# A hybrid diffusion layer on one core: TensorE's recurrence loop written out, and two small moves around it

## The reference, cut to what matters

```python
def wkv7_scan(r, w, k, v, a, b, s0, reverse):
    def step(S, inp):
        r_t, w_t, k_t, v_t, a_t, b_t = inp
        sa = jnp.einsum('bhvk,bhk->bhv', S, a_t)
        S = S * w_t[:, :, None, :] + sa[..., :, None] * b_t[..., None, :] + v_t[..., :, None] * k_t[..., None, :]
        return S, jnp.einsum('bhvk,bhk->bhv', S, r_t)
    ...
for d in range(2):
    ...
    kd = kh * (1.0 + (a - 1.0) * k_a)
    y, s_fin = wkv7_scan(rh, decay, kd, vh, -kk, kk * a, s0[d], reverse=(d == 1))
```

## Time and profile before

| | |
|---|---|
| time, median of three runs | 2733.13 us |
| the profiled execution's own time | 2725.9 us |
| its span (first to last instruction) | 2724.2 us |
| TensorE busy | 2289.1 us (84%), 26342 matmuls |
| VectorE busy | 1612.5 us (59%) |
| ScalarE busy | 1036.5 us (38%) |
| GpSimd busy | 233.0 us (9%) |
| mean granted TensorE clock | 0.931 |

### The profile page before, as it was taken

The page is one execution under the profiler, slowest core; times in us unless marked ns, Lnnn a source line. Parts: engine busy times, 40 slices in busy tenths (PEclk is TensorE's granted clock), DMA queues, the critical chain, the costliest instruction groups (busy, mean ns, idle before and its releaser), DMA issues. The chain is left out here.

```text
span 2724.2 us, 65696 instructions
## 1 busy us (share of the span) xinstructions
PE 2289.1 (84%) x26342; PEld 1857.7 (68%) x26342; DVE 1612.5 (59%) x2511; ACT 1036.5 (38%) x1760; POOL 233.0 (9%) x192
## 2 busy tenths in 40 slices
PE   5999999998999999996777777774553796798898
PEld 3788788886888888884666666663342574687687
DVE  6665665668654566664665666654675575677233
ACT  5443244444321244443444454442322664200222
POOL 0000000000000000003110001000000640200421
PEclk7999999999999999997899999997776898899899
DMA  6344333332333333332011111104335304676543
GB/s 217 115 134 121 93 116 118 102 119 96 111 100 98 97 116 102 114 107 79 28 44 37 37 37 37 48 23 133 125 119 162 118 3 129 235 265 236 177 139 123
DMA packets 263884, 300.23 MB, mean 110 GB/s; under 512 B 33274, under 2 KB 203386, under 8 KB 255482
## 3 DMA queue, kind: packets, MB, share of 16 engines
q1 hardware_dynamic: 261370, 288.65, 32.9%
q10 hardware_dynamic: 2304, 8.39, 0.8%
HBM read 194.62 MB, written 102.36 MB: 109 GB/s over the span
## 5 line engine op out<-in xcount | busy, mean ns | idle before, releaser
L715 PE MATMUL proj_ps<-h_hi,w_hi 128*128 128x512 f32 x1656 | 650.0, 393 | 28.2 <-DVE h_lo L465 20.3
L716 PE MATMUL proj_ps<-h_lo,w_hi 128*128 128x512 f32 x1656 | 647.3, 391 | 0.0
L717 PE MATMUL proj_ps<-h_hi,w_lo 128*128 128x512 f32 x1656 | 647.2, 391 | 0.0
L318 ACT CAST w_hi<-w_raw 128x512 fp32r<-128x512 f32 x420 | 255.1, 621 | 695.7 <-PE proj_ps L717 353.2
L715 PEld LDWEIGHTS proj_ps<-h_hi,w_hi 128*128 128x128 f32 x1656 | 312.6, 189 | 98.7 <-issue 27.2
L717 PEld LDWEIGHTS proj_ps<-h_hi,w_lo 128*128 128x128 f32 x1656 | 312.4, 189 | 65.9
L716 PEld LDWEIGHTS proj_ps<-h_lo,w_hi 128*128 128x128 f32 x1656 | 312.7, 189 | 63.4
L482 DVE TENSOR_TENSOR w_lo<-w_raw,w_hi 128x512 fp32r<-128x512 f32 x420 | 283.2, 689 | 44.0 <-ACT w_hi L318 43.7
L498 DVE TENSOR_TENSOR z_slots<-proj_ps,x_rows 128x512 f32<-128x512 f32 x174 | 120.3, 691 | 171.0 <-PE proj_ps L717 169.0
L498 DVE TENSOR_TENSOR x_rows<-proj_ps,x_rows 128x512 f32<-128x512 f32 x116 | 80.2, 691 | 109.7 <-PE proj_ps L717 103.8
L967 POOL TENSOR_TENSOR neighbours<-z_halo 128x1792 f32<-128x1792 f32 x9 | 28.8, 3200 | 1268.7 <-DMA z_halo<-scratch_zT 1268.7
(11 more groups left out here) (333 smaller groups left out, 3992.9 us busy)
## 6 DMA issues: line engine op xcount, KB each, us to landing
w_raw<-in_w_in SPq DMA_DIRECT2D x240, 256.0 KB, 3.0
scratch_gatesT<-z_slots SPq DMA_DIRECT2D x128, 256.0 KB, 2.7
m_gate<-scratch_gatesT SPq DMA_DIRECT2D x32, 1024.0 KB, 5.7
scratch_zT<-z_slots SPq DMA_DIRECT2D x108, 256.0 KB, 2.5
ada<-in_ada_w SPq DMA_DIRECT2D x4, 2048.0 KB, 15.4
mb_raw<-scratch_branchT SPq DMA_DIRECT2D x16, 512.0 KB, 5.6
scratch_mergedT<-m_y SPq DMA_DIRECT2D x8, 1024.0 KB, 5.7
y_raw<-scratch_mergedT SPq DMA_DIRECT2D x16, 512.0 KB, 4.9
```

The source lines that it names most:

```text
L318: A.copy(wh[:, i, :, :], raw[:, q, :, :]).then_inc(w_hi, 1)
L715: T.matmul(out, wh[:, i, k, :], hi[:, o, k, :], start=(first and k == 0), stop=False, skip_group_check=not first)
L716: T.matmul(out, wh[:, i, k, :], lo[:, o, k, :], start=False, stop=False, skip_group_check=not first)
L717: last = T.matmul(out, wl[:, i, k, :], hi[:, o, k, :], start=False, stop=(k == 3), skip_group_check=not first)
```

## The change

Four edits. TensorE no longer uses `units`: its program is 18 units in a row. VectorE's two halves of the states are split: the first half (P0, Q0) stays at the end of the unit, the second half (P1, Q1) comes behind the level-one mask of the next unit. TensorE's wait for Q1 moves accordingly, from ahead of X to between X and Z of level one. The turned rows of K in direction one move from level 3 to behind level 5, into PSUM bank 6, and ScalarE's copy of them moves behind the last Z. The names of the results are split to match (`tail_v`).

```diff
+            def states(n, d, c):
+                main_p.after(dve, n, f"PQ.{d}")
+                prep_a.after(dve, n, f"tot{d}")
...
+                done(V.tensor_tensor(to(Pst), pq[:, :, 0, :, :], eye, ALU.add), "P")
+                done(V.tensor_tensor(to(Qst), pq[:, :, 1, :, :], tt.to_broadcast([P, 2, 2, CH]), ALU.mult), "Q")
...
                     if v == 1:
+                        if d:
+                            states(n, 0, 1)
+                        elif not first_block(n):
+                            states(n - 1, 1, 1)
...
                 if nxt:
                     first_inverse(*nxt)
-                for c in range(2):
...
+                states(n, d, 0)
+                if nxt is None:
+                    states(n, d, 1)
```

ScalarE:

```diff
-                rows(Kt if d else Vt, "Kt." if d else "V.", "K." if d else "V.")
+                if d == 0:
+                    rows(Vt, "V.", "V.", 7)
...
                 factor(Z[:], "Z5.", 0)
-                if d == 0:
-                    rows(Kt, "Kt.", "K.")
+                rows(Kt, "Kt.", "K.", 6 if d else 7)
```

TensorE:

```diff
                         main_a.after(pe, n, f"Bt.{d}")
-                        if d:
-                            turned(lambda p: Kh[:, d, p, :], "K.")
-                        else:
+                        if d == 0:
                             turned(lambda p: zf[:, 4 + p, :], "V.")
...
-                        main_a.after(pe, n, f"Kt.{d}" if d else f"V.{d}")
+                        if d == 0:
+                            main_a.after(pe, n, "V.0")
...
                     if v == 1:
                         main_g.after(pe, n, f"Z.{d}")
                         before(main_a, "Y1.")
-                        before(main_v, "Q1.")
...
                         done(last, f"X{v}.")
+                    if v == 1:
+                        before(tail_v, "Q1.")
+                        go()
...
                 if d == 0:
                     prep_v.after(pe, n, "bt")
                     prep_p.done(mm(ps[:, 6, :], J[:], flat(kds[:])), "bonus")
+                else:
+                    turned(lambda p: Kh[:, d, p, :], "K.", 6)
                 main_a.after(pe, n, f"Z5.{d}")
...
                     if d == 0:
                         prep_v.after(pe, n, "bonus")
-                        main_a.after(pe, n, "Kt.0")
+                    main_a.after(pe, n, f"Kt.{d}")
                     first_inverse(*nxt)
...
-            units(pe, prologue, unit)
+            prologue()
+            for n in range(NBLK):
+                unit(n, 0, (n, 1))
+                unit(n, 1, (n + 1, 0) if n + 1 < NBLK else None)
```

More of the change, by code:

```diff
@@ L887, in recurrence_local_stage @@
         main_v = Results(ctx, nc, "main_vector", [f"{n}{d}" for d in range(2) for n in
-                         ["G1.", "MK.", "G2.", "G3.", "G4.", "G5.", "Gs0.", "Gs1.", "P0.", "Q0.", "P1.", "Q1."]])
+                         ["G1.", "MK.", "G2.", "G3.", "G4.", "G5."]])
+        tail_v = Results(ctx, nc, "tail_vector", [f"{n}{d}" for d in range(2) for n in ["Gs0.", "Gs1.", "P0.", "Q0.", "P1.", "Q1."]])
         head_v = Results(ctx, nc, "head_vector", ["MB.0", "X0.0", "MB.1", "X0.1"])
@@ L894, in recurrence_local_stage @@
         main_a = Results(ctx, nc, "main_scalar", [f"{n}{d}" for d in range(2) for n in
-                         ["X1.", "Z1.", "X2.", "Z2.", "Bt.", "X3.", "Z3.", "Kt." if d else "V.", "At.", "X4.", "Z4.", "MV.", "Z5."]
-                         + ["Kt."] * (1 - d) + ["W0.", "W1.", "Y0.", "Y1."]])
+                         ["X1.", "Z1.", "X2.", "Z2.", "Bt.", "X3.", "Z3."] + ["V."] * (1 - d)
+                         + ["At.", "X4.", "Z4.", "MV.", "Z5.", "Kt.", "W0.", "W1.", "Y0.", "Y1."]])
         prep_p = Results(ctx, nc, "prep_products", ["tw0", "ta0", "ks", "rnT", "tw1", "ta1", "bonus"])
         main_p = Results(ctx, nc, "main_products", [f"{n}{d}" for d in range(2) for n in
-                         ["G1.", "SK.", "X1.", "Z1.", "G2.", "B.", "X2.", "Z2.", "G3.", "K." if d else "V.", "X3.", "Z3.",
-                          "G4.", "A.", "X4.", "Z4.", "G5.", "MV."] + ["K."] * (1 - d) + ["Z5.", "W.", "GY.", "PQ."]])
+                         ["G1.", "SK.", "X1.", "Z1.", "G2.", "B.", "X2.", "Z2.", "G3."] + ["V."] * (1 - d) + ["X3.", "Z3.",
+                          "G4.", "A.", "X4.", "Z4.", "G5.", "MV."] + ["K.", "Z5."][::1 - 2 * d] + ["W.", "GY.", "PQ."]])
         head_p = Results(ctx, nc, "head_products", ["SB.0", "SM.0", "SB.1", "SM.1"])
@@ L943, in turn @@
                         load(n + 2)
-                    main_v.after(sp, n, f"Gs1.{d}")
+                    tail_v.after(sp, n, f"Gs1.{d}")
                     sp.dma_start(t["gT"][d, :, :, bass.ds(n * RB, RB)].rearrange("m p t -> p m t"), gst[:]).then_inc(g_stored, 16)
@@ L1121, in prologue @@
                     consts_set.step(dve, V.tensor_tensor(lev[:, d, 1:, :], lev[:, d, 1:, :], ident, ALU.add))
+            def states(n, d, c):
+                main_p.after(dve, n, f"PQ.{d}")
+                prep_a.after(dve, n, f"tot{d}")
+                done = lambda ins, name: tail_v.done(ins, f"{name}{c}.{d}")
+                pq = ps[:, c, :].rearrange("p (g q m j) -> p g q m j", g=2, q=2, m=2)
+                to = lambda st: st[:, d, bass.ds(n * 4, 4), :, :].rearrange("p (g c) m j -> p g c m j", c=2)[:, :, c, :, :]
+                tt = tot[:, d, bass.ds(n * 4, 4), :].rearrange("p (g c) (m o) -> p g c m o", c=2, o=1)[:, :, c, :, :]
+                eye = i64[:, :].rearrange("p (a b j) -> p a b j", a=1, b=1).to_broadcast([P, 2, 2, CH])
+                done(V.tensor_tensor(to(Pst), pq[:, :, 0, :, :], eye, ALU.add), "P")
+                done(V.tensor_tensor(to(Qst), pq[:, :, 1, :, :], tt.to_broadcast([P, 2, 2, CH]), ALU.mult), "Q")
             def unit(n, d, nxt):
@@ L1163, in unit @@
                     of_chunk = lambda a: a.rearrange("p m (g c t) -> p c g m t", g=2, c=2)[:, c]
-                    done(V.tensor_tensor(of_chunk(gst[:]), ps[:, 4 + c, 0:256].rearrange("p (g m t) -> p g m t", g=2, m=2),
-                                         of_chunk(AR[:, d, 1, :, :]), ALU.add), f"Gs{c}.")
+                    tail_v.done(V.tensor_tensor(of_chunk(gst[:]), ps[:, 4 + c, 0:256].rearrange("p (g m t) -> p g m t", g=2, m=2),
+                                         of_chunk(AR[:, d, 1, :, :]), ALU.add), f"Gs{c}.{d}")
                 if nxt:
                     first_inverse(*nxt)
-                main_p.after(dve, n, f"PQ.{d}")
-                prep_a.after(dve, n, f"tot{d}")
-                for c in range(2):
[L1171 to L1176, removed]
+                states(n, d, 0)
+                if nxt is None:
+                    states(n, d, 1)
             units(dve, prologue, unit)
@@ L1241, in factor, with rows @@
                     own(A.copy(to.rearrange("p q g m t -> p q (g m t)"), ps[:, bank:bank + 2, 0:256]), name)
-                def rows(to, name, sent):
+                def rows(to, name, sent, bank):
                     main_p.after(act, n, f"{sent}{d}")
-                    own(A.copy(flat(to[:]), ps[:, 7, :]), name)
+                    own(A.copy(flat(to[:]), ps[:, bank, :]), name)
                 if nxt and d:
@@ L1257, in unit @@
                 factor(Z[:], "Z2.", 0)
-                rows(Bt, "Bt.", "B.")
+                rows(Bt, "Bt.", "B.", 7)
                 if nxt and d:
@@ L1361, in before, with turned @@
                         results.earlier(pe, n, f"{name}1")
-                def turned(src, name):
+                def turned(src, name, bank=7):
                     for g in range(2):
@@ L1366, in turned @@
                             at = g * 256 + p * P
-                            last = T.transpose(ps[:, 7, at:at + P], src(p)[:, g * P:(g + 1) * P], s["ident"][:])
+                            last = T.transpose(ps[:, bank, at:at + P], src(p)[:, g * P:(g + 1) * P], s["ident"][:])
                     done(last, name)
```

## The result

The changed kernel took 2714.24 us (median of five, 2711.13 to 2717.56) beside 2733.13 us of the kernel before: ratio 0.9925, 95% interval 0.9907 to 0.9944, so 15 to 25 us, 20.5 by the ratio. Forecast: 2708, range 2688 to 2726. The profiled execution took 2714.24 us, that of before 2725.9: the two traces differ by 11.7 us only.

What follows compares the result with a forecast made beforehand. TensorE was taken as bound by its instruction supply, packets of some 256 about 3.3 to 4.3 us apart. Terms 16 + 5 + 3.5 = 24.5 us off the median 2733.1 gave 2708.6, forecast 2708, range 2688 to 2726.

Steps and rivals of the forecast that it cites:

- Part A: TensorE's loop written out, removing six back-edge jumps and no matmul: 16 us faster.
- Part B: States' second half moved behind the level-one mask, so TensorE waits less for VectorE's mask: 5 us faster.
- The clock's price: Granted clock falls behind each back-edge jump of TensorE's loop: 0.55 us per jump, 3.3 in all.
- a sign that I named: "Issue", TensorE's idle time waiting for nothing visible, 54.8 us in the loop's six pairs, lower by about 10 to 20.
- My upper bound: For Part A: all 20.3 us idle at the jumps goes, with the clock's price 23.6; 30 allowed.
- the lower bound: For Part B, TensorE's level-one mask waits: a gain of 0.
- Part C: Direction one's four K transposes leave level 3 for TensorE's idle time behind level 5: 3.5 us faster.
- R1: Written-out pairs idle like the first; packets swallow half the rest of Part B and Part C: 6 us, 2727; chance 0.16.
- R3: TensorE's stops vanish in written-out code: 67 us faster, 2666; chance 0.02.
- R4: Written-out packets come later from new addresses; at 0.9 us each the kernel is 24 us slower, 2757; chance 0.05.
- R5: Later stages' loops lie otherwise against packets' ends, possibly 3.4 us a turn; 8 us each way in the width.

Runs made afterwards that it cites:

- `micro`: Kernel before plus 2048 unread 64x64 products in TensorE's prologue, 1024 in a 16-turn loop, 1024 written out; profiled execution 2798.94 us.
- `a_only`: Kernel before with only TensorE's loop written out, VectorE and TensorE keeping their old order; 2713.49 us, ratio 0.992.
- the loop's experiment: Kernel before, loop kept, with only the states' second half moved behind level one's mask and TensorE's wait for Q1 with it; ratio 0.9994.
- `ac_out`: Changed kernel without the states' move: loop written out and K's rows moved; ratio 0.9902 against the kernel before.
- `ab_out`: Changed kernel with K's rows back at level 3: loop written out and states' move; ratio 0.9936 against the kernel before.

## Why the prediction was right or wrong

The direction, the range and the engine were right: 2714.24 in 2688 to 2726, 18.9 us by the medians where 24.5 were summed. The terms were less so: A was some 6 us too low and B at least 5 too high, and that these errors cancelled is luck.

- **What bounds the kernel.** Right, and measured alone by `micro`: instruction packets, one per 3.45 to 4.0 us where the code is dense, as the earlier trace rows had let me read (3.31 to 4.33), and 256 instructions to a packet, one weight load to a matmul (26342 of each on the page of before). Where TensorE waits for other engines, an end can pass without a stop: in the six pairs of `a_only` 10299 matmuls and 10293 weight loads are 80 packets, and it has 41 stops for "issue".
- **Part A, 16 us.** Too small: 22 (18 to 25) by the ratio. The term is the difference of two pairs in one trace, 62.0 and 59.35 us. Its written-out side was right: a pair of `a_only` takes 355.93 / 6 = 59.3 us, so between the two traces the stretch shrank by 16.1 us. What was mis-sized is the loop's side: it came from one execution, 7.2 us below the median of its five runs and 9 below that of the 29, and the sum carried this over as if it were a constant. In the other kernels with the loop, which have edits of their own, a pair took 62.2 to 64.1 us.
- **Part A, the mechanism.** Right in part. The idle time at the jumps went, 20.3 to 6.4 us, but the sum of the stops fell by 6.6 only; 10.7 us came out of TensorE's busy time. The clock's price, in the bounds, was too low: I took the difference of two units' lengths, 0.55 us for each jump, 3.3 in all, though the shorter one held an idle stretch of its own, 1.28 us before its X. The busy times in the same rows, 24.15 and 22.41, differ by 1.74, 10.4 for six jumps. How the 22 us divide between stops and clock stays open. Also, a sign that I named was the wrong one to look for: "issue" was to be lower by 10 to 20 us, and it was lower by 6.6 with A alone and by 1.6 with all. My upper bound, "all the idle time at the jumps goes", treated those stops as apart from the rest.
- **Part B, 5 us.** Wrong: it brought nothing, and written out it rather cost. The sentence that should have been carried through is in the prediction: "where a packet is late, TensorE reaches its end earlier and stands there longer". I halved the gain for it. The whole level-one stretch lies in code where a packet's 128 matmuls take 2.09 us of a packet's 3.5 to 4, so the lower bound, 0, was the value to take, and the loop's experiment agrees with it. Below 0 I had only the price of a wait that X covers. X does cover it in the trace above, Q1 out at 1364.50 and Z reached at 1366.21, and the kernels with B are still 4 us or more behind.
- **Part C, 3.5 us.** Right as far as the runs tell: 5 us (2 to 8) in the loop, 3 to 5 written out, there within the noise. The idle 0.79 us behind level 5 took the transposes in: the wait for `inv_t` there is down from 4.7 to 1.2 us in six pairs.
- **The rivals.** R1 (packets give it back) was right in its mechanism: B was given back wholly, and in the traces two thirds of the jumps' 20.3 us ("issue" fell from 54.8 to 48.2 in `a_only`). It was wrong on A's worth. R3, no stops, is excluded. R4, slower packets from new addresses: of its sign, stops longer than 2.5 us, `a_only` has 2.6 at the most and `ac_out` one of 3.1, and both are faster; excluded as a price that decides. R5, side effects in later stages: from the chain's first product to the end the trace of before has 860.5 us (from 1863.73 on) and that after 861.9 (from 1850.63 on), within the 8 us that I allowed. In the other written-out kernels it is 854.8 to 863.2.

## What to carry to other kernels

Where TensorE's small matmuls run back to back over several packets of code, ask of every saved wait whether the next packet is there: here only the gain in sparser code passed through (in the loop C's 5 us, nothing of B). Count a jump's price by what follows it (here the granted clock, 0.50 behind one) as well as by the idle time before it, and take the pair that is to be changed from more than one execution. And a change of a few us in a loop with a long body can be its layout (6 and 12 us for shifts by 60 and 90 here): shift it by some instructions before believing either sign.

## What the runs showed of the hardware that was not expected

- 128 matmuls of 64x64 tiles with their weight loads, fp32, take 2.09 us and arrive 3.45 to 4.00 us apart when written out (`micro`); in a loop with a body of 128 they run at 17.5 ns each without a stop.
- Shifts of a loop's body by 60, 90 and 150 instructions that do nothing cost 6, 12 and 14 us, of the last about 4 for the instructions themselves, and it has five packets fewer (175 against 180).
- A wait of 0.51 us for VectorE taken out of dense matmul code came back as a longer stop at the next packet's end, 0.61 us against 0.20 (`a_only`, `ab_out`).
